# Long convolution over 256 positions: second half kept reversed, no mirror product, inverse products of 128 columns, even and odd parts combined on VectorE

## Chip, cores and metric

One core of one Trainium2 chip runs the whole program. The metric is the device time of one execution in microseconds (us). The kernel before took 1390.03 us (median of three executions, 1386.08 to 1390.8).

## The reference, cut to what matters

The program computes two trunk layers on 128 prompt tokens and 256 sample tokens. Layer 0 mixes the tokens by a state-space scan and, beside it, by an order-2 "Hyena": a short convolution gives three parts of 1024 channels each, and two long convolutions over the whole sequence are gated by parts 1 and 2:

```python
def long_conv(u, h, bias):
    L = u.shape[1]
    U = jnp.fft.rfft(uf, n=2 * L, axis=1)
    Hf = jnp.fft.rfft(h.astype(jnp.float32), axis=0)
    y = jnp.fft.irfft(U * Hf[None], n=2 * L, axis=1)[:, :L]
    return (y + uf * bias.astype(jnp.float32)).astype(u.dtype)
...
    parts = jnp.split(dwconv_centred(hy, hy_conv_w, hy_conv_b), 1 + HY_ORDER, axis=-1)
    filters = hyena_filters(L, hy_w1, hy_b1, hy_w2, hy_b2, hy_w3, hy_freq)
    u = parts[0]
    for o in range(HY_ORDER):
        u = parts[o + 1] * long_conv(u, filters[:, o], hy_bias[o])
    return jnp.concatenate([y, u], axis=-1) @ w_out, final
```

After it come the output projection, a mixture of experts (router, gather, 16 pairs of experts), a second layer of attention, and a second mixture of experts.

## The kernel before

Data are held with channels on partitions: `u0T`, `p1T` and `hyT` are the three Hyena parts, eight chunks of 128 channels by 384 positions (prompt 0 to 127, sample 128 to 383). The program is written out per engine; semaphores are counted. `bank_plan` (L115) lists in TensorE's order every result that goes through one of the 8 PSUM banks, with the engine that takes it out; `open_bank` (L841) makes TensorE wait until the bank's former content is taken, `full` and `took` (L632, L636) are the waits for "TensorE has finished this job" and "its taker has read it". All matmuls are issued by `mm` (L851) and all transposes by `tr` (L855), so the profile shows them under these two lines. A float32 `mm` is two recorded MATMULs, a `tr` is one. `link` issues an instruction on VectorE and waits for its end before the next; a plain instruction is not waited for.

The long convolution is done by products with constant cosine matrices, in four turns, one for each (half of the channels b, order o) in `HYO`: (0,0), (1,0), (0,1), (1,1). Per turn TensorE does this (L1125 to L1187, loop L1227):

- `spectrum`: 6 products of 512 columns from the token-major inputs `ut` (2 for the prompt, 4 for the sample);
- for the next turn `tokens` (12 transposes into banks 6, 7 and again 6, which ScalarE copies to `ut`) and `filters` (6 products, copied out by ScalarE and then multiplied by a decay on GpSimd, L2636), and among the filters `mirror`: one product of 512 columns with a flipped identity, that reverses the second sample half;
- `prompt_back`: 8 products of 128 columns, once VectorE has the prompt's spectrum (`spec`);
- for the next turn `prompt_response`: 2 products of 512 columns;
- `sample_back`: 16 products of 256 columns into banks 2 and 3, once VectorE has all three spectra;
- for the next turn `sample_response`: 4 products of 512 columns.

VectorE per turn (L2325): `spectrum` three times (6 instructions on 128x512, L2307 to L2313), `mirror` (L2275, L2276: second half plus and minus the first), `gate` on the prompt (L2320), `prompt_response` (L2281), `gate` twice on the sample, one for each bank, and `sample_response` (5 instructions, L2285 to L2295). In the last turn TensorE has no next turn to prepare and does `first_states`, 16 products of the output projection, in that place.

Ahead of the turns, 24 chunks of the Hyena projection are convolved with three taps on VectorE (L2248 to L2251; the third tap is one instruction per segment). SyncE's queue starts the first expert weights when jobs of the last turn are done (`LAST_UTK` L742, `LAST_SPEC_S`, `LAST_INV` L758), the rest as experts are used (L770); GpSimd's queue waits for `LAST_INV` at L2639.

Of the kernel before, what the change touches and what calls it, by code (L numbers as in the profile page):

```python
# [114 lines left out]
def bank_plan():  # L115
# [81 lines left out]
    def tokens(b, o):  # L197
        for t, bank in ((0, 6), (2, 7), (1, 6)):
            job(("utk", b, o, t), "act", None, bank)

    def filters(b, o):
        for i, (s, x, t) in enumerate(HY_FILTERS):
            job(("PQ", b, o, s, x, t), "act", None, (7, 6, 1)[i % 3])
            if i == 0 and (b, o) != HYO[0]:
                job(("rev", b, o), "dve", None, 0)

    for turn in range(-1, len(HYO)):
        if turn >= 0:
            b, o = HYO[turn]
            for s in range(2):  # L210
                for k in range(s + 1):
                    job(("U", b, o, s, k, 0), "none", None, 2 * (s + k))
                    job(("U", b, o, s, k, 1), "dve", None, 2 * (s + k) + 1)
            if turn + 1 < len(HYO):
                tokens(*HYO[turn + 1])
                filters(*HYO[turn + 1])
            job(("inv", b, o, 0, 0), "dve", None, 7)
        else:
            tokens(*HYO[0])
        if turn + 1 < len(HYO):  # L220
            job(("H", *HYO[turn + 1], 0), "dve", None, 6)
            job(("H", *HYO[turn + 1], 1), "act", None, 1)
            if turn < 0:
                job(("rev", *HYO[0]), "dve", None, 0)
# [129 lines left out]
def host_constants():  # L354
# [15 lines left out]
    def halves(n):  # L370
# [9 lines left out]
        back = [w.T / (2 * n) for pair in both for w in pair]  # L380
# [8 lines left out]
    def feat(n):  # L389
# [29 lines left out]
            "k_slots": slots, "k_small": small, "k_rev": rev, "k_flip": rev / 8, "k_pick": pick}  # L419
# [5 lines left out]
def build_kernel(nc, A, K, outs):  # L425

    with ExitStack() as ctx:
# [103 lines left out]
        dft = area(16384, 2560)  # L531
        dft0 = dft[:, 0:512].rearrange("p (x n) -> p x n", x=4)
        dft1 = dft[:, 512:1536].rearrange("p (x n) -> p x n", x=8)
        dft1_back = dft[:, 1536:2560].rearrange("p (x n) -> p x n", x=4)
# [6 lines left out]
        flip = hyl[0][:, 3584:3584 + P]  # L541
# [85 lines left out]
        def wide(h):  # L627
            return slice(h * 512, (h + 1) * 512)
        done = S("pe_done")
# [208 lines left out]
        def _(pe):  # L838
# [286 lines left out]
            def tokens(b, o):  # L1125
# [3 lines left out]
                for t in (0, 2, 1):  # L1129
# [5 lines left out]
            def mirror(b, o):  # L1135
                ps = open_bank("rev", b, o)
                took(pe, "utk", b, o, 2)
                mm(ps[:, :], flip, ut[:, 2, :], True, True).then_inc(done, 1)

            def filters(turn, b, o):  # L1140
                for i, (s, x, t) in enumerate(HY_FILTERS):
                    ps = open_bank("PQ", b, o, s, x, t)
                    mm(ps[:, :], (hsP, hsQ)[x][:, cols(s + t)], w3s[:, b, o, :], True, True).then_inc(done, 1)
                    if i == 0 and turn:
                        mirror(b, o)
# [13 lines left out]
            def spectrum(b, o):  # L1159
# [4 lines left out]
                took(pe, "rev", b, o)  # L1164
# [13 lines left out]
            def sample_back(turn, b, o):  # L1178
                pe.wait_ge(S("spec"), 3 * turn + 3)
                for i in range(2):  # L1180
                    ps = open_bank("inv", b, o, 1, i)
                    for c in range(2):
                        for k in range(2):
                            for x in range(2):
                                last = mm(ps[:, c * LS:(c + 1) * LS], yspec[1 + k][:, x, cols(2 * i + c)], dft1_back[:, 2 * k + x, :],
                                          k == x == 0, k == x == 1)
                    last.then_inc(done, 1)  # L1187

            for q in range(3):
                for c in range(KD):  # L1190
# [19 lines left out]
                    if ("hy", q, c) == FILTERS_AFTER:  # L1210
                        pe.wait_ge(S("hs"), 1)
                        pe.wait_ge(S("hypar0_in"), 16 * 6)
# [12 lines left out]
            mirror(*HYO[0])  # L1225
# [345 lines left out]
        def _(act):  # L1571
# [197 lines left out]
            for c in range(3 * KD):  # L1769
# [13 lines left out]
                if (c // KD, c % KD) == GATES_AFTER:  # L1783
# [4 lines left out]
                    for l in range(2):  # L1788
                        act.dma_start(gates_d[l].rearrange("g v (c p) -> c (g v) p", p=P),
                                      gstage[0:KD, l, :].rearrange("c (i p) -> c i p", p=P)).then_inc(S("gates_out"), 16)  # L1790
            act.wait_ge(S("gates_out"), 16 * 2)
            for turn, (b, o) in enumerate(HYO):
                for t in (0, 2, 1):
# [11 lines left out]
                A_(gsin, bank("G", b, o, 2)[:, :], ACT.Copy).then_inc(taken["act"], 1)  # L1805

# [190 lines left out]
        def _(dve):  # L1997
# [245 lines left out]
            for c in range(3 * KD):  # L2243
# [72 lines left out]
            def gate(b, o, s, i):  # L2316
                full(dve, "inv", b, o, s, i)
                c, n = (b * 4, 4) if s == 0 else (b * 4 + 2 * i, 2)
                dst = (p1T if o == 0 else hyT)[:, c:c + n, SEGS[s][0]:SEGS[s][1]]
                take(TT(dst, dst, bank("inv", b, o, s, i)[:, :].rearrange("p (c n) -> p c n", c=n), mult))  # L2320
# [4 lines left out]
            for turn, (b, o) in enumerate(HYO):  # L2325
# [6 lines left out]
                gate(b, o, 0, 0)  # L2332
# [242 lines left out]
        def _(pool):  # L2575
# [53 lines left out]
            pool.wait_ge(S("hypar0_in"), 16 * 6)  # L2629
# [159 lines left out]
```

## Time and profile before

| | |
|---|---|
| median of three executions | 1390.03 us |
| lowest, highest | 1386.08, 1390.8 us |
| span of the profiled execution, first to last instruction | 1382.9 us |
| device time of the profiled execution itself | not given beside its span |
| TensorE busy over the span | 88% |
| VectorE, ScalarE, GpSimd busy | 33%, 24%, 14% |

The span leaves out what lies around the first and the last instruction: the median is 7.1 us above it, the lowest time 3.2 us. A row of a timeline gives start, duration, engine, line, operation, "output<-inputs" by buffer name, and count; a bracket gives the idle time before it and what ended that. Merged rows (x12) are of equal instructions in a row. `arena`, `ring`, `hT`, `scr`, `rstd` are regions of SBUF, `bank` is PSUM.

### The profile page before, as it was taken

The numbers are of one execution on the slowest core, as the hardware profiler recorded it, in microseconds if no ns is written. First come the engines' busy times: TensorE is split into PE (matmuls) and PEld (weight loads), VectorE is DVE, ScalarE is ACT, GpSimd is POOL, SyncE is SP. The second block draws the span as 40 slices with busy tenths as digits, with TensorE's granted clock in tenths as the row PEclk, the third lists the DMA queues.
The fourth block names the chain that finished last, engine by engine and source line by source line (L and its number), as shares of the span: only waits on it lengthen the run. The fifth ranks groups of instructions, "written<-read, shape, count | busy, mean of one in ns | idle before, by whom it ended". The sixth has DMA issues, their size and how long they took to land.

```text
span 1382.9 us, 16600 instructions
## 1 busy us (share of the span) xinstructions
PE 1221.0 (88%) x6381; PEld 689.0 (50%) x6381; DVE 457.1 (33%) x958; ACT 329.9 (24%) x843; POOL 191.6 (14%) x253
## 2 busy tenths in 40 slices
PE   3999998999989999959999875999888969989773
PEld 2456654454545664446555441853455446545431
DVE  1452078542338850241111114212363331111105
ACT  4112364210122200231111113313353221111103
POOL 1000022200123401011221200152001011212100
PEclk9999999999999999979999997999999979999996
DMA  9995510666910118259999995950314469999983
GB/s 332 323 387 209 182 31 1 225 242 248 349 60 1 61 51 332 83 180 391 418 418 417 420 411 222 354 56 7 137 62 124 182 229 416 419 419 419 419 369 146
DMA packets 94417, 337.23 MB, mean 244 GB/s; under 512 B 12784, under 2 KB 16598, under 8 KB 69649
## 3 DMA queue, kind: packets, MB, share of 16 engines
q1 hardware_dynamic: 73472, 303.18, 56.2%
q0 software_dynamic: 13984, 26.19, 6.8%
q10 hardware_dynamic: 6897, 6.97, 1.5%
q8 instruction: 45, 0.74, 0.2%
q14 instruction: 19, 0.16, 0.0%
HBM read 334.08 MB, written 23.18 MB: 258 GB/s over the span
## 4 chain that ended last, share of the span: by engine, by line
PE 71%; DMA 17%; DVE 6%; ACT 3%; issue 2%; POOL 1%; SPq 0%; ACTq 0%; DVEq 0%; POOLq 0%
PE bank L851 63%; DMA ring<-in_moe_w_down_dram 10%; PE bank L855 5%; DMA ring<-in_moe_w_up_dram 3%; PE bank L882 3%; DMA arena<-expert_rows 1%; DMA xR<-in_x_sample_dram 1%; DVE arena L2477 1%; PE bank L948 1%; ACT ring L1963 1%; DVE arena L2480 1%; DMA hT<-rows,scr 0%; DMA arena<-in_hy_freq_dram 0%; ACT rstd L1598 0%; DMA expert_rows<-arena,scr 0%
## 5 line engine op out<-in xcount | busy, mean ns | idle before, releaser
L851 PE MATMUL bank<-ring,arena 128*64 128x256 f32 (+3 forms) x2624 | 438.5, 439 | 43.9 <-DMA ring<-in_moe_w_up_dram 17.4
L851 PEld LDWEIGHTS bank<-ring,arena 128*64 128x64 f32 (+1 forms) x2624 | 218.2, 146 | 229.8 <-issue 120.2
L851 PE MATMUL bank<-hT,ring 128*128 128x384 f32 (+5 forms) x968 | 306.1, 474 | 4.3 <-ACT hT L1670 3.6
L851 PEld LDWEIGHTS bank<-hT,ring 128*128 128x128 f32 (+1 forms) x968 | 180.1, 193 | 125.7 <-issue 19.1
L851 PE MATMUL bank<-arena 128*64 128x256 f32 (+7 forms) x800 | 117.2, 383 | 11.2 <-DVE arena L2425 4.5
L2452 DVE TENSOR_TENSOR hT<-hT,bank 128x256 f32<-128x256 f32 x32 | 13.5, 421 | 266.8 <-ACT hT L1850 266.8
L851 PEld LDWEIGHTS bank<-arena 128*64 128x64 f32 (+4 forms) x800 | 60.2, 150 | 53.4 <-issue 29.6
L1850 ACT ACTIVATE hT<-bank 128x256 f32<-128x256 f32 x32 | 12.3, 384 | 248.4 <-PE bank L851 248.4
L855 PEld LDWEIGHTS bank<-cst,hT 128*128 128x128 f32 x368 | 47.4, 190 | 48.0 <-issue 35.9
L855 PE MATMUL bank<-cst,hT 128*128 128x128 f32 x368 | 61.1, 301 | 11.3 <-DMA hT<-rows,scr 11.3
L855 PE MATMUL bank<-cst,arena 128*128 128x128 f32 (+3 forms) x207 | 31.9, 302 | 37.7 <-ACT arena L1611 19.3
L851 PE MATMUL bank<-ring,hT 128*128 128x512 f32 x144 | 62.7, 594 | 0.4 <-ACT hT L1977 0.4
L851 PE MATMUL bank<-arena,ring 128*128 128x256 f32 (+3 forms) x272 | 60.0, 373 | 3.2 <-ACT arena L1926 1.8
L2457 DVE COPY arena<-bank 128x512 f32<-128x512 f32 x32 | 22.1, 691 | 111.6 <-PE bank L851 111.6
L851 PEld LDWEIGHTS bank<-arena,ring 128*128 128x128 f32 (+2 forms) x272 | 41.5, 184 | 23.9 <-issue 9.2
L855 PEld LDWEIGHTS bank<-cst,arena 128*128 128x128 f32 (+3 forms) x207 | 26.5, 157 | 48.5 <-issue 39.9
L851 PE MATMUL bank<-arena,cst 128*128 128x512 f32 (+5 forms) x76 | 37.2, 645 | 12.4 <-DVE arena L2398 9.4
L1861 ACT ACTIVATE arena<-bank 128x512 f32<-128x512 f32 x32 | 19.1, 597 | 114.6 <-PE bank L851 114.6
L851 PEld LDWEIGHTS bank<-ring,hT 128*128 128x128 f32 x144 | 27.1, 190 | 33.8 <-issue 33.2
L2675 POOL DMA_INDIRECT hT<-rows,scr x32 | 33.0, 1030 | 71.8 <-PE bank L855 27.9
L2691 POOL COPY scr<-arena 128x1 int32 x28 | 5.1, 183 | 271.1 <-ACT arena L1861 164.5
L2681 POOL DMA_INDIRECT expert_rows<-arena,scr x32 | 32.7, 1020 | 59.8 <-POOL scr L2691 23.5
(305 smaller groups left out, 1120.2 us busy)
## 6 DMA issues: line engine op xcount, KB each, us to landing
ring<-in_moe_w_up_dram SPq DMA_DIRECT2D x28, 2048.0 KB, 21.0
ring<-in_moe_w_down_dram SPq DMA_DIRECT2D x28, 2048.0 KB, 20.1
ring<-in_w_ada_dram SPq DMA_DIRECT2D x24, 2048.0 KB, 15.2
ring<-in_moe_w_gate_dram SPq DMA_DIRECT2D x24, 2048.0 KB, 21.0
ring<-in_ev_w_in_dram SPq DMA_DIRECT2D x11, 2048.0 KB, 11.7
arena<-in_moe_w_gate_dram SPq DMA_DIRECT2D x8, 2048.0 KB, 14.4
ring<-in_ev_w_out_dram SPq DMA_DIRECT2D x4, 2048.0 KB, 15.8
arena<-in_moe_w_up_dram SPq DMA_DIRECT2D x4, 2048.0 KB, 19.0
```

Of the source, the lines that this page charges most:

```text
L851: return nc.tensor.matmul(out, lhsT, rhs, start=start, stop=stop_, skip_group_check=True)
L855: return nc.tensor.transpose(out, in_, ident[0:n, 0:n])
L882: last = nc.tensor.matmul(ps[32 * g:32 * g + 32, :], conds[l][:, k, at:at + 32], w[:, k, :], start=b == first and k < 4, stop=(l, b) in AD ...
L948: last = nc.tensor.matmul(ps[32 * q:32 * q + 32, :], conds[0][:, k, 22 - 2 * j:54 - 2 * j], w[:, k, :], start=j == 0 and k < 4, stop=j == ...
L1861: A_(ob[:, 0:512], banks[5][:, :], ACT.Copy).then_inc(s["d_act"], 1)
L1963: A_(prob[b][:, a, 0:w], bank("score", n, a)[:, 0:w], ACT.Exp, bias=nrows[:, b, 1, a:a + 1], scale=scale, accum_out=nrows[:, b, 2, a:a + 1 ...
L2452: TT(hid[:, b, :], sg[:, b, :], banks[2 + b][:, HID:2 * HID], mult).then_inc(s["hid"], 1)
L2457: COPY(ob[:, 512:1024], banks[6][:, :]).then_inc(s["d_dve"], 1)
L2477: link(STT(out=y0, in0=y1, scalar=ysw[:, NT + t:NT + t + 1], in1=y0, op0=mult, op1=add))
L2480: weighed = TT(y0, y0, bank("gff", l, v, h), mult)
L2675: nc.gpsimd.indirect_dma_start(xs[:, b, :], None, rows_d[l], bass.IndirectOffsetOnAxis(ap=at, axis=0), bounds_check=T - 1, oob_is_err=False)\
L2681: nc.gpsimd.indirect_dma_start(outs_d[l], bass.IndirectOffsetOnAxis(ap=idxc[:, 2 + b:3 + b], axis=0), ob, None, bounds_check=2 * T - 1, oo ...
```

## The change

The sample's second half of parts 0 and 1 is written backwards by the third tap of the short convolution, which becomes three instructions. So no mirror product is needed: the middle block of tokens is transposed in the place where `mirror` stood, into bank 0, and VectorE adds and subtracts straight from it. The even and the odd frequencies' inverse products are kept apart (8 products of 128 columns each): ScalarE copies the odd part to the new region `mirrored`, and VectorE forms even+odd (first half) and even-odd (second half, reversed) and multiplies each with the gate, for o = 1 through an access pattern that walks backwards. The constant `k_flip` and its DMA go, and half of the inverse matrices.

```diff
     def tokens(b, o):
-        for t, bank in ((0, 6), (2, 7), (1, 6)):
+        for t, bank in ((0, 6), (2, 7)):
...
             if i == 0 and (b, o) != HYO[0]:
-                job(("rev", b, o), "dve", None, 0)
+                job(("utk", b, o, 1), "dve", None, 0)
...
-                job(("inv", b, o, 1, i), "dve", None, 2 + i)
+                job(("inv", b, o, 1, i), ("act", "dve")[i], None, 2 + i)
...
-        back = [w.T / (2 * n) for pair in both for w in pair]
+        back = [w[:h].T / (2 * n) for pair in both for w in pair]
...
+        def backwards(ap):
+            step, n = ap.ap[-1]
+            return bass.AP(ap.tensor, ap.offset + step * (n - 1), [*ap.ap[:-1], [-step, n]])
...
-            def mirror(b, o):
-                ps = open_bank("rev", b, o)
-                took(pe, "utk", b, o, 2)
-                mm(ps[:, :], flip, ut[:, 2, :], True, True).then_inc(done, 1)
+            def middle_tokens(b, o):
+                src = u0T if o == 0 else p1T
+                ps = open_bank("utk", b, o, 1)
+                for c in range(4):
+                    last = tr(ps[:, cols(c)], src[:, b * 4 + c, cols(1)])
+                last.then_inc(done, 1)
...
-                    for c in range(2):
+                    for c in range(4):
                         for k in range(2):
-                            for x in range(2):
-                                last = mm(ps[:, c * LS:(c + 1) * LS], yspec[1 + k][:, x, cols(2 * i + c)], dft1_back[:, 2 * k + x, :],
-                                          k == x == 0, k == x == 1)
+                            x = (k + 1 - i) % 2
+                            last = mm(ps[:, cols(c)], yspec[1 + k][:, x, cols(c)], dft1_back[:, 2 * k + x, :], k == 0, k == 1)
...
+            def take_odd(b, o):
+                full(act, "inv", b, o, 1, 0)
+                A_(mirrored, bank("inv", b, o, 1, 0)[:, :], ACT.Copy).then_inc(taken["act"], 1)
...
                 A_(him[0], bank("H", b, o, 1)[:, :], ACT.Copy).then_inc(taken["act"], 1)
+                if turn:
+                    take_odd(*HYO[turn - 1])
                 full(act, "G", b, o, 2)
...
-                for v, (a, b) in enumerate(SEGS):
-                    last = STT(out=dst[:, a:b], in0=src[:, 2 + a + v:2 + b + v], scalar=col("hy_conv_w", 6 * KD + c),
-                               in1=acc[:, a + v:b + v], op0=mult, op1=add)
+                for v, (a, b) in enumerate(SEGS if q == 2 else (SEGS[0], (LP, 2 * P), (2 * P, T))):
+                    to, v = dst[:, a:b], min(v, 1)
+                    last = STT(out=backwards(to) if q < 2 and a == 2 * P else to, in0=src[:, 2 + a + v:2 + b + v],
+                               scalar=col("hy_conv_w", 6 * KD + c), in1=acc[:, a + v:b + v], op0=mult, op1=add)
...
             def mirror(b, o):
-                full(dve, "rev", b, o)
-                took(dve, "utk", b, o, 1)
-                ps = bank("rev", b, o)[:, :]
-                link(TT(ut[:, 2, :], ut[:, 1, :], ps, sub))
-                take(TT(ut[:, 1, :], ut[:, 1, :], ps, add))
+                full(dve, "utk", b, o, 1)
+                took(dve, "utk", b, o, 2)
+                ps = bank("utk", b, o, 1)[:, :]
+                link(TT(ut[:, 1, :], ps, ut[:, 2, :], add))
+                take(TT(ut[:, 2, :], ps, ut[:, 2, :], sub))
...
+            def sample_gate(b, o):
+                full(dve, "inv", b, o, 1, 1)
+                took(dve, "inv", b, o, 1, 0)
+                even = bank("inv", b, o, 1, 1)[:, :]
+                dst = (p1T if o == 0 else hyT)[:, 4 * b:4 * b + 4, :]
+                near, far = dst[:, :, cols(1)], dst[:, :, cols(2)]
+                if o == 1:
+                    far = backwards(far)
+                link(TT(ytmp[:, :], even, mirrored, add))
+                link(TT(mirrored, even, mirrored, sub))
+                TT(near, near, by_chunk(ytmp[:, :]), mult)
+                take(TT(far, far, by_chunk(mirrored), mult))
...
-                for i in range(2):
-                    gate(b, o, 1, i)
+                sample_gate(b, o)
...
-                    dma(flip, K["k_flip"]).then_inc(S("hypar0_in"), 16)
```

## Rows read from the trace of the kernel before

**Rows 1.** The page: span, and busy time of each engine.

```profile
span 1382.9 us, 16600 instructions
...
PE 1221.0 (88%) x6381; PEld 689.0 (50%) x6381; DVE 457.1 (33%) x958; ACT 329.9 (24%) x843; POOL 191.6 (14%) x253
```

**Rows 2.** Window, one turn: length, busy of each engine, PEclk, DMA, GB/s.

```profile
415.97:442.94 26.97, 26.72 (x100) 16.27 (x98) 21.48 (x30) 6.46 (x11) 8.39 (x6) 1.00 0.00 1
```

**Rows 3.** Timeline, TensorE and ScalarE, first turn.

```profile
415.97 1.04 PE L855 MATMUL bank<-cst,arena 128*128 128x128 f32 x8
...
416.61 1.09 ACT L1795 ACTIVATE hT<-bank 128x512 f32<-128x512 f32 x2 [5.85 <-PE bank L855]
...
417.75 1.12 PE L851 MATMUL bank<-ring,arena 128*128 128x512 f32 x2
...
418.71 1.02 PE L851 MATMUL bank<-hT,ring 128*128 128x512 f32 x2
...
419.57 4.45 PE L851 MATMUL bank<-ring,arena 128*128 128x512 f32 x10
...
423.86 1.95 PE L851 MATMUL bank<-arena,ring 128*128 128x128 f32 x16
...
425.64 1.88 PE L851 MATMUL bank<-hT,arena 128*128 128x512 f32 x4
...
427.36 7.16 PE L851 MATMUL bank<-arena,ring 128*128 128x256 f32 x32
...
434.36 3.60 PE L851 MATMUL bank<-arena 128*128 128x512 f32 x8
...
437.79 5.31 PE L851 MATMUL bank<-hT,arena 128*128 128x512 f32 x12
```

**Rows 4.** Timeline, VectorE, first turn.

```profile
412.84 0.69 DVE L2307 TENSOR_TENSOR ring<-bank,hT 128x512 f32<-128x512 f32 x1 [0.33 <-PE bank L851]
...
416.93 0.69 DVE L2307 TENSOR_TENSOR ring<-bank,arena 128x512 f32<-128x512 f32 x1
...
425.74 1.55 DVE L2313 TENSOR_TENSOR ring<-ring,rstd 128x512 f32<-128x512 f32 x1
427.32 0.69 DVE L2275 TENSOR_TENSOR hT<-hT,bank 128x512 f32<-128x512 f32 x1
428.05 0.69 DVE L2276 TENSOR_TENSOR hT<-hT,bank 128x512 f32<-128x512 f32 x1
428.65 0.68 DVE L2320 TENSOR_TENSOR arena<-arena,bank 128x512 f32<-128x512 f32 x1
...
434.56 0.69 DVE L2320 TENSOR_TENSOR arena<-arena,bank 128x512 f32<-128x512 f32 x1 [2.77 <-PE bank L851]
```

**Rows 5.** Timeline, the entry into the first turn.

```profile
403.30 0.65 PE L855 MATMUL bank<-cst,arena 128*128 128x128 f32 x4 [0.31 <-ACT hT L1795]
...
404.74 1.10 PE L851 MATMUL bank<-scr,arena 128*128 128x512 f32 x2 [0.78 <-ACT hT L1795]
```

**Rows 6.** One line's instructions: L2309 on VectorE; GpSimd's timeline in the first turn.

```profile
L2309 DVE TENSOR_TENSOR ring<-ring,rstd x12: 691/692/1602, 414.2 to 503.2; 128x512 f32<-128x512 f32 x12
...
422.55 5.87 POOL L2636 TENSOR_TENSOR arena<-arena,ring 128x512 f32<-128x512 f32 x4
```

**Rows 7.** Timeline, last turn; a chunk of the short convolution.

```profile
496.83 13.90 PE L851 MATMUL bank<-ring,arena 128*128 128x512 f32 x32
...
309.30 0.48 DVE L2248 TENSOR_SCALAR arena<-arena,par 128x385 f32<-128x385 f32 x1 [3.24 <-ACT arena L1755]
```

**Rows 8.** SyncE's queue; windows behind the turns (columns as in rows 2).

```profile
621.62 0.37 SPq L765 DMA_DIRECT2D arena<-in_moe_w_gate_dram  x1
...
760.00:822.00 62.00, 49.55 (x360) 26.73 (x356) 6.73 (x13) 6.93 (x16) 9.16 (x15) 1.00 1.01 418
610.00:620.00 10.00, 2.17 (x73) 2.04 (x72) 4.71 (x19) 0.00 (x0) 2.12 (x2) 0.50 0.12 34
990.00:1000.00 10.00, 8.61 (x70) 5.67 (x68) 6.82 (x21) 5.36 (x20) 0.00 (x0) 1.00 0.33 96
```

More of the change, by code:

```diff
@@ L530, in build_kernel @@
         hacc = area(13072, 2, PADDED - 2)
-        dft = area(16384, 2560)
+        dft = area(16384, 2048)
         dft0 = dft[:, 0:512].rearrange("p (x n) -> p x n", x=4)
         dft1 = dft[:, 512:1536].rearrange("p (x n) -> p x n", x=8)
-        dft1_back = dft[:, 1536:2560].rearrange("p (x n) -> p x n", x=4)
+        dft1_back = dft[:, 1536:2048].rearrange("p (x n) -> p x n", x=4)
+        mirrored = area(18432, 512)
         hsP, hsQ = area(18944, T), area(19328, T)
@@ L540, in build_kernel @@
         hyb = hyl[1][:, 0:2048].rearrange("p (b o n) -> p b o n", b=2, o=2)
-        flip = hyl[0][:, 3584:3584 + P]
         hy_lent = ring[:, HY_LENT * SLOT:(HY_LENT + 1) * SLOT]
@@ L1128, in tokens @@
                     took(pe, "inv", b, 0, 1, 1)
-                for t in (0, 2, 1):
+                for t in (0, 2):
                     ps = open_bank("utk", b, o, t)
@@ L1144, in filters @@
                     if i == 0 and turn:
-                        mirror(b, o)
+                        middle_tokens(b, o)
             def prompt_response(turn, b, o):
@@ L1163, in spectrum @@
                     mm(ps[:, :], dft0[:, x, :], ut[:, 0, :], True, True).then_inc(done, 1)
-                took(pe, "rev", b, o)
+                took(pe, "utk", b, o, 1)
                 for k in range(2):
@@ L1211, in _ @@
                         pe.wait_ge(S("hs"), 1)
-                        pe.wait_ge(S("hypar0_in"), 16 * 6)
+                        pe.wait_ge(S("hypar0_in"), 16 * 5)
                         filters(0, *HYO[0])
@@ L1224, in _ @@
             prompt_response(0, *HYO[0])
-            mirror(*HYO[0])
+            middle_tokens(*HYO[0])
             sample_response(0, *HYO[0])
@@ L1790, in _ @@
                                       gstage[0:KD, l, :].rearrange("c (i p) -> c i p", p=P)).then_inc(S("gates_out"), 16)
+            def take_odd(b, o):
+                full(act, "inv", b, o, 1, 0)
+                A_(mirrored, bank("inv", b, o, 1, 0)[:, :], ACT.Copy).then_inc(taken["act"], 1)
             act.wait_ge(S("gates_out"), 16 * 2)
             for turn, (b, o) in enumerate(HYO):
-                for t in (0, 2, 1):
+                for t in (0, 2):
                     full(act, "utk", b, o, t)
@@ L1805, in _ @@
                 A_(gsin, bank("G", b, o, 2)[:, :], ACT.Copy).then_inc(taken["act"], 1)
+            take_odd(*HYO[-1])
             def moe(l):
@@ L2314, in spectrum, with by_chunk, prompt_gate @@
                 dve.wait_ge(S("spec"), 3 * turn + i + 1)
[L2316 to L2320, printed above, removed]
+            def by_chunk(ap):
+                return ap.rearrange("p (c n) -> p c n", c=4)
+            def prompt_gate(b, o):
+                full(dve, "inv", b, o, 0, 0)
+                dst = (p1T if o == 0 else hyT)[:, 4 * b:4 * b + 4, cols(0)]
+                take(TT(dst, dst, by_chunk(bank("inv", b, o, 0, 0)[:, :]), mult))
+            def sample_gate(b, o):
[10 more added lines that the diff above has]
+                take(TT(far, far, by_chunk(mirrored), mult))
             prompt_response(*HYO[0])
@@ L2331, in _ @@
                     mirror(*HYO[turn + 1])
-                gate(b, o, 0, 0)
+                prompt_gate(b, o)
                 if more:
                     prompt_response(*HYO[turn + 1])
-                for i in range(2):
-                    gate(b, o, 1, i)
+                sample_gate(b, o)
                 if more:
@@ L2627, in _ @@
                 dma(decay[b], K["k_decay"][:, :, b * 512:(b + 1) * 512].rearrange("t p n -> p t n")).then_inc(S("hypar%d_in" % which), 16)
-            pool.wait_ge(S("hypar0_in"), 16 * 6)
+            pool.wait_ge(S("hypar0_in"), 16 * 5)
             for turn, (b, o) in enumerate(HYO):
```

4 lines of the change are left out of this document (2 added, 2 removed).

## The prediction

> **What bounds the kernel now.** I read the page's engine line first: TensorE is busy 88% of the span, VectorE 33% [rows 1]. So a product taken away on TensorE is worth its time, unless something else is late in that place. The place is the four turns of the long convolution, and the windows by turn come next: a turn is 26.97 us long and TensorE is busy 26.7 of it, while VectorE is busy 21.5 [rows 2]. The reader is to see that VectorE has only 5.5 us of room in a turn, and that the change gives work to it. The timelines of one turn then show who waits for whom: in the first turn VectorE finishes its last spectrum at 425.74+1.55 = 427.29 [rows 4] and TensorE starts the sample's inverse products at 427.36 [rows 3], which is also where its own preceding products end (425.64 + 4 x 0.43). The two engines arrive together. After that VectorE waits for TensorE, 2.77 us in one piece before the second sample gate [rows 4].
>
> **The change on TensorE.** A stage ends where the next row starts, since the ends of matmuls are modelled.
>
> Inverse products: 32 passes of 256 columns from 427.36 to 434.36, 7.00 us, 0.219 each [rows 3]. After: 16 products are again 32 passes, but of 128 columns. The trace has this very form, with the same operands' regions, in the prompt's inverse: 16 passes from 423.86 to 425.64, 1.78 us, 0.111 each [rows 3]. So 3.56 us, 3.44 less in each of four turns, 13.76 in all. The Trainium skill (TensorE: Matmul & The Clock Gate, Back-to-back issue gap) gives about 81 ns for one of a stream of 128-column matmuls; the row has 111 ns for a float32 pass. By the page these 32 passes would take 2.6 us and a turn would save 0.96 more where TensorE binds. I go by the row.
>
> Mirror: it occupies 418.71 to 419.57, 0.86 us [rows 3]. In its place come 4 transposes; eight take 1.04 us and four 0.65, both with the same tail [rows 3, 5], so four are about 0.41. That is 0.45 less. The place they leave among the tokens gives nothing: the first filter product goes into bank 7 and needs ScalarE's second copy, which ends at 416.61+1.09 = 417.70, and it starts at 417.75 [rows 3]. It will start then with or without the middle transposes.
>
> Entry to the first turn: the middle transposes start at 403.30, after a wait for ScalarE's copy, and the first response product at 404.74, again after a wait for a copy [rows 5]. Without them the response product can start at 403.30: 1.44 less, and 0.45 for the mirror, 1.89.
>
> If all that counted, the sum would be 13.76 + 3 x 0.45 + 1.89 = 17.0 us.
>
> **The change on VectorE.** Call T the start of the sample's inverse products. Before, VectorE gates the first bank while the second is computed. After, the gate needs both parts, so it waits for the last product; behind it stand, in order, the next turn's sample response and its three spectra, and for the last spectrum waits TensorE's next T. That is a loop through both engines:
> - product seen at T + 3.56 + 0.20 (before: 434.36 to 434.56 [rows 3, 4]);
> - four instructions in place of two: an instruction that is waited for takes 0.72 to the next start, one that is not 0.60 (427.32, 428.05, 428.65 [rows 4]): 2 x 0.72 + 2 x 0.60 = 2.64. The last two multiply SBUF by SBUF, which no gate did before; nearest rows 0.69 us alone and 1.60 beside GpSimd [rows 6]. GpSimd ends its six products about 1 us after T (422.55+5.87 = 428.42 against 427.36 [rows 3, 6]), before they start. I take 0.60;
> - sample response: five instructions by the same step of 0.72, 3.60, if TensorE doesn't hold it up; it does so before, not after, as its four products start at T + 3.56 already;
> - three spectra. One alone takes 412.84 to 416.93, 4.09, three 12.3; the trace has 14.45 (412.84 to 427.29) [rows 4], since L2309 and L2313 read two SBUF operands and take up to 1.55 to 1.60 instead of 0.69 while GpSimd works [rows 4, 6]. The Trainium skill (SBUF — State Buffer, Who interferes with whom) has the rule: a VectorE instruction with two SBUF inputs and a GpSimd instruction that reads SBUF exclude each other, and the later waits for the whole of the other; these rows agree with it. The cost now is three hits, 2.15 us. After, the spectra of turns 1 and 2 start later against TensorE's filters, so GpSimd starts about 5.8 us after them and not 6.8. Six GpSimd products of 1.25 let one VectorE instruction in after every two, so again three hits, but each with nearly a full wait of 0.95: 15.1 us. Bounds: no hit 12.3, all six instructions hit 18.0;
> - 0.07 until TensorE starts.
>
> Sum 3.76 + 2.64 + 3.60 + 15.1 + 0.07 = 25.2 us, against 26.97 before: 1.78 less per turn. TensorE itself would be ready at T + 3.56 (inverse) + 3.43 (response) + 5.15 (434.36 and 437.79 to 442.94 [rows 2, 3]) + 1.78 (tokens until the first filter) + 0.86 + 0.41 + 4.29 + 1.78 + 1.72 = 23.0. So TensorE, gapless before, will wait about 2.2 us before the inverse products of turns 1 and 2.
>
> By turns, from the first T to the end:
> - turn 0: its spectra start when TensorE's first product pair is done, 1.89 earlier (VectorE is ready 0.2 before). With GpSimd's second product 0.45 earlier they take some 0.35 longer, 14.8: T comes 1.5 earlier;
> - turns 1 and 2: 2 x 1.78 = 3.56;
> - from turn 2's T to the end of turn 3: two inverse stages shorter, 6.88. Here `first_states`, 32 passes from 496.83 to 510.56 [rows 7], covers VectorE, whose spectra without GpSimd end at about T + 22.3, before TensorE asks at T + 26.
>
> Sum 1.5 + 3.56 + 6.88 = 11.9, taken as **12 us**.
>
> **Edits at nothing.** ScalarE's copy of the odd part (0.60) starts at T + 2.0 and is over at T + 2.6, while the gate waits until T + 3.76 for the even part; behind it on ScalarE stands only the sine copy, whose product is done at T + 6.1. If the copy were late the gate would wait for it one for one. The third tap in three pieces adds one VectorE instruction, 0.35 to 0.5 us, to 16 chunks, where VectorE is idle 3.24 us in a chunk [rows 7]; a write that walks backwards is in no row, its bounds being the 0.35 of a forward one and the longest row, 1.60, both under the idle time. The backward gates of o = 1 (turns 2 and 3) stand ahead of work that `first_states` or the output projection covers. The Trainium skill (DVE: opcode table, Instruction layouts) allows negative steps and gives no price. The flip DMA and the smaller matrix shorten a queue nobody waits for. `LAST_UTK` moves behind one filter product, 0.9 us later for a load into an empty queue.
>
> **What comes behind.** SyncE issues the next loads when jobs of the last turn are done, and the load at 621.62 after the gather; both follow TensorE and move with it [rows 8]. From there the DMA queues are full, share 1.01 at 418 GB/s while TensorE has gaps [rows 8]. Such a stretch has a fixed length but starts when it is triggered, so I count the 12 us in full behind it.
>
> On the profiled execution's span of 1382.9 this is 1370.9; the median stands 7.1 above the span: 1390.0 - 12.0 = **1378.0 us**.
>
> **Rivals.**
> 1. TensorE stays the bound: if contention with GpSimd vanishes (spectra 12.3, loop 22.4 under TensorE's 23.0), all 17.0 count: 1373.0. For it: VectorE is idle 5.5 us per turn. Against: that idle time lies behind TensorE's long inverse, which goes. Chance 0.14.
> 2. Given back later: the expert weights set the end of the mixture, and if their transfers can't start earlier a large part of the 12 goes. For it: share 1.01. Against: every trigger moves. With two thirds lost, 1386. Chance 0.12.
> 3. Contention at its worst, all six hits: loop 28.1, 1.1 more per turn, turn 0 1.7 more, and 6.88 saved: 3.0 less, 1387. It needs GpSimd busy in the whole of the spectra; its six products fill half. Chance 0.05.
> 4. Slower: the clock. TensorE's new waits of about 2 us could drop its granted clock to 1.2 GHz, as in the window 610 to 620, where it was busy 2.17 of 10 us and was granted 0.50 [rows 8]. If the 7.0 us of inverse and response behind each of three waits ran at half speed they would cost 21 in all: 1399. It decides from 4 us per turn on. Against: between 990 and 1000, with 1.4 us of waits in it (busy 8.61 of 10), the granted clock is 1.00 [rows 8]. The Trainium skill (TensorE: Matmul & The Clock Gate, Part 1) says that the clock follows how busy TensorE has been, so this is the rule that speaks against the change. Chance 0.05.
>
> **Numbers.** The forecast has 0.64, with 1375.5 to 1381 as its own range. The range 1373 to 1384 takes in rival 1, most of the bounds of the contention, and part of rival 2. Within 0.3% (4.2 us) a change can't be told from none. Faster: the forecast, rival 1 and about half of rival 2, 0.85; same: the rest of 2 and rival 3, 0.10; slower 0.05.
>
> **What would show it.** Right: sample inverse products 32 passes in 3.6 us; TensorE waiting for L2313's successor about 2 us in turns 1 and 2, about 1 in turn 0 and none in turn 3; turns of about 25 us; VectorE with hardly any idle time but the wait for the even part. Wrong: passes at 0.219, turns of 23 us or of over 26, a granted clock below 1.00 between 400 and 510, or a wait for weights behind 700 that has grown by as much as was saved.

## Result and the profile after

| | before | after |
|---|---|---|
| median | 1389.4 us (4 runs, 1386.08 to 1390.8) | 1375.79 us (4 runs, 1373.8 to 1378.57) |
| ratio | | 0.99, 95% interval 0.9873 to 0.9926 |
| profiled execution: device time / span | not given / 1382.9 | 1374.37 / 1372.4 us |
| TensorE, VectorE busy over the span | 88%, 33% | 88%, 34% |

The change is faster by 13.6 us of medians, 1.0%, and the interval of the ratio leaves out 1; a second set of runs, below, gave 0.9904 (0.9887 to 0.992). The forecast was 1378.0. The two profiled spans lie only 10.5 us apart. The median of before stands 6.5 above its span, while a single execution's time lies about 2 us above its own span (1374.37 over 1372.4; 1.6 to 3.1 in all executions that have both). So some 4.5 us between span and median of before was spread between executions: its profile comes from one of the shorter ones.

To see where the time comes from, the stage of the four turns is measured by the starts of TensorE's rows, which the spread of the rest of the program does not touch. As in the prediction, T is the start of a turn's sample inverse products, and the entry is the way from the first token transposes to the first turn's spectrum. The columns: whole stage, from its first token transposes to the end of its last inverse product; T0, from the same start to the first T; the next two turns, T to T; the rest; and the lowest granted clock in windows of 2 us over the entry.

| kernel | stage | T0 | turns | rest | clock |
|---|---|---|---|---|---|
| before | 117.36 | 25.46 | 26.97, 26.95 | 37.98 | 1.00 |
| after | 106.43 | 25.36 | 24.87, 24.85 | 31.35 | 0.50 |

The first view is the timeline of after, TensorE, from the entry to the second turn. `mm` is now L855 and `tr` L859.

```profile
401.29 1.09 PE L859 MATMUL bank<-cst,arena 128*128 128x128 f32 x8 [2.66 <-DVE arena L2264]
402.78 1.52 PE L855 MATMUL bank<-scr,arena 128*128 128x512 f32 x2 [0.40 <-ACT hT L1804]
404.10 1.91 PE L855 MATMUL bank<-rstd,arena 128*128 128x512 f32 x2
405.80 1.06 PE L859 MATMUL bank<-cst,arena 128*128 128x128 f32 x4
...
426.65 3.84 PE L855 MATMUL bank<-arena,ring 128*128 128x128 f32 x32 [0.24 <-DVE ring L2326]
430.33 3.60 PE L855 MATMUL bank<-arena 128*128 128x512 f32 x8
433.76 5.31 PE L855 MATMUL bank<-hT,arena 128*128 128x512 f32 x12
438.92 1.04 PE L859 MATMUL bank<-cst,arena 128*128 128x128 f32 x8
440.69 1.12 PE L855 MATMUL bank<-ring,arena 128*128 128x512 f32 x2 [0.74 <-ACT hT L1804]
...
451.52 2.72 PE L855 MATMUL bank<-arena,ring 128*128 128x128 f32 x22 [1.47 <-DVE ring L2326]
```

The reader is to see three things. The 32 inverse passes of 128 columns take 430.33 - 426.65 = 3.68 us where [rows 3] had 7.00. A wait for VectorE stands before them, 1.47 us in turn 1 (0.24 in turn 0), where before the two engines arrived together. And at the entry the products run at half speed: the second response product's two passes of 512 columns take 405.80 - 404.10 = 1.70 us from start to start, and in the kernel before 0.86:

```profile
405.67 1.02 PE L851 MATMUL bank<-rstd,arena 128*128 128x512 f32 x2
406.53 1.02 PE L851 MATMUL bank<-hT,ring 128*128 128x512 f32 x2
```

VectorE in after, from the gate of turn 0 to the last spectrum of turn 1:

```profile
430.53 0.69 DVE L2345 TENSOR_TENSOR rstd<-bank,arena 128x512 f32<-128x512 f32 x1 [1.28 <-PE bank L855]
...
432.59 0.68 DVE L2348 TENSOR_TENSOR arena<-arena 128x512 f32<-128x512 f32 x1
433.19 0.68 DVE L2298 TENSOR_TENSOR ring<-bank,ring 128x512 f32<-128x512 f32 x1
...
436.56 0.68 DVE L2320 TENSOR_TENSOR ring<-bank,hT 128x512 f32<-128x512 f32 x1
...
444.02 1.62 DVE L2326 TENSOR_TENSOR ring<-ring,rstd 128x512 f32<-128x512 f32 x1
...
447.00 1.55 DVE L2322 TENSOR_TENSOR ring<-ring,rstd 128x512 f32<-128x512 f32 x1
...
449.92 1.55 DVE L2326 TENSOR_TENSOR ring<-ring,rstd 128x512 f32<-128x512 f32 x1
451.50 0.69 DVE L2288 TENSOR_TENSOR hT<-bank,hT 128x512 f32<-128x512 f32 x1
```

From 430.53 to 451.50 VectorE never stops, and three instructions that read two SBUF operands take 1.55 to 1.62 us in place of 0.69. Such a long one is called a hit below. The windows of the same kernel, turns 1 and 2 and the rest (length, busy of TensorE, weight load, VectorE, ScalarE, GpSimd, granted clock, DMA):

```profile
426.65:451.52 24.87, 22.66 (x97) 13.37 (x97) 22.97 (x32) 6.87 (x12) 9.45 (x7) 1.00 0.00 1
451.52:476.37 24.85, 22.65 (x96) 13.36 (x97) 22.95 (x32) 6.47 (x11) 8.35 (x6) 1.00 0.23 85
476.37:507.72 31.35, 31.35 (x132) 18.91 (x133) 20.98 (x32) 2.76 (x4) 0.00 (x0) 1.00 0.07 21
```

Against [rows 2] TensorE is no longer busy all the time (22.66 of 24.87; the 2.21 us are 1.47 of waiting for VectorE and 0.74 for ScalarE's copy of the tokens), with the granted clock at 1.00 all the same. The last window is gapless.

### The profile page after: what moved, and what is told of

It is laid out like the page before. It is cut to its first block, busy times and chain, and to the rows that moved or that the text cites. A ratio compares the mean times of both kernels' runs of the same rounds, so it can differ in the third digit from the quotient of the medians.

```text
span 1372.4 us, 16607 instructions
## 1 busy us (share of the span) xinstructions
PE 1206.8 (88%) x6373; PEld 677.9 (49%) x6373; DVE 464.7 (34%) x982; ACT 329.9 (24%) x843; POOL 191.3 (14%) x252
## 4 chain that ended last, share of the span: by engine, by line
PE 68%; DMA 17%; DVE 9%; ACT 3%; issue 2%; POOL 1%; SPq 0%; ACTq 0%; DVEq 0%; POOLq 0%
PE bank L855 60%; DMA ring<-in_moe_w_down_dram 10%; PE bank L859 5%; DMA ring<-in_moe_w_up_dram 4%; PE bank L886 3%; DMA arena<-expert_rows 1%; DVE ring L2326 1%; DVE ring L2322 1%; DMA xR<-in_x_sample_dram 1%; PE bank L952 1%; ACT ring L1975 1%; DMA hT<-rows,scr 0%; ACT rstd L1603 0%; DVE rstd L2324 0%; DVE ring L2320 0%
## 5 line engine op out<-in xcount | busy, mean ns | idle before, releaser
L855 PE MATMUL bank<-ring,arena 128*64 128x256 f32 (+3 forms) x2624 | 438.1, 438 | 46.4 <-DMA ring<-in_moe_w_up_dram 17.8
L855 PEld LDWEIGHTS bank<-ring,arena 128*64 128x64 f32 (+1 forms) x2624 | 217.7, 146 | 230.8 <-issue 117.9
L855 PE MATMUL bank<-hT,ring 128*128 128x384 f32 (+4 forms) x960 | 302.9, 474 | 4.3 <-ACT hT L1675 3.6
L855 PEld LDWEIGHTS bank<-hT,ring 128*128 128x128 f32 (+1 forms) x960 | 178.6, 193 | 123.9 <-issue 17.2
L855 PE MATMUL bank<-arena 128*64 128x256 f32 (+7 forms) x800 | 117.3, 383 | 10.6 <-DVE arena L2452 4.5
L855 PEld LDWEIGHTS bank<-arena 128*64 128x64 f32 (+4 forms) x800 | 60.0, 151 | 52.1 <-issue 29.1
L859 PEld LDWEIGHTS bank<-cst,hT 128*128 128x128 f32 x368 | 47.4, 190 | 48.1 <-issue 35.9
L859 PE MATMUL bank<-cst,hT 128*128 128x128 f32 x368 | 61.1, 301 | 11.4 <-DMA hT<-rows,scr 11.4
L859 PE MATMUL bank<-cst,arena 128*128 128x128 f32 (+3 forms) x207 | 32.7, 308 | 37.0 <-ACT arena L1616 19.8
L855 PE MATMUL bank<-ring,hT 128*128 128x512 f32 x144 | 63.2, 597 | 0.4 <-ACT hT L1989 0.4
L855 PE MATMUL bank<-arena,ring 128*128 128x128 f32 (+2 forms) x272 | 46.8, 324 | 6.4 <-DVE ring L2326 3.2
L859 PEld LDWEIGHTS bank<-cst,arena 128*128 128x128 f32 (+3 forms) x207 | 27.6, 160 | 49.5 <-issue 42.8
L855 PE MATMUL bank<-arena,cst 128*128 128x512 f32 (+5 forms) x76 | 36.4, 632 | 12.4 <-DVE arena L2425 9.4
L855 PEld LDWEIGHTS bank<-ring,hT 128*128 128x128 f32 x144 | 27.3, 192 | 34.3 <-issue 33.5
L855 PEld LDWEIGHTS bank<-arena,ring 128*128 128x128 f32 (+2 forms) x272 | 32.1, 185 | 24.6 <-issue 9.2
## 6 DMA issues: line engine op xcount, KB each, us to landing
ring<-in_w_ada_dram SPq DMA_DIRECT2D x24, 2048.0 KB, 15.1
```

Of the source, the lines that this page charges most:

```text
L855: return nc.tensor.matmul(out, lhsT, rhs, start=start, stop=stop_, skip_group_check=True)
L859: return nc.tensor.transpose(out, in_, ident[0:n, 0:n])
```

## The experiments

Eleven runs, all with a profile. The totals of single executions scatter by some 5 us (the four spans of after ran from 1371.9 to 1376.6) and do not follow the stage from run to run, so the stage is what the experiments are read by; a second run of after gave the stage as 106.44 and its turns as 24.85 and 24.87. The last column is the total; it is a median of 5 executions for "all" and of 6 for "after again", and a single execution elsewhere.

| kernel | stage | T0 | turns | rest | clock at the entry | total |
|---|---|---|---|---|---|---|
| inverse only | 104.67 | 25.46 | 23.92, 23.94 | 31.35 | kept | 1375.0 |
| reversed only | 118.10 | 26.27 | 26.90, 26.91 | 38.02 | fell | 1388.89 |
| small decay | 100.79 | 23.29 | 23.13, 23.13 | 31.24 | kept | 1375.16 |
| filled entry | 104.77 | 23.68 | 24.87, 24.87 | 31.35 | kept | 1376.33 |
| spectrum in PSUM | 102.48 | 24.97 | 23.13, 23.13 | 31.25 | fell | 1371.11 |
| dummy in mirror's place | 104.08 | 24.87 | 23.92, 23.94 | 31.35 | fell | 1379.44 |
| all | 98.26 | 22.44 | 22.29, 22.28 | 31.25 | kept | 1368.32 |
| after again | 106.44 | 25.37 | 24.85, 24.87 | 31.35 | fell | 1375.12 |
| PSUM and filler | 100.79 | 23.28 | 23.13, 23.13 | 31.25 | kept | 1374.49 |
| mirror kept, PSUM | 104.73 | 26.39 | 23.55, 23.55 | 31.24 | fell | 1372.67 |
| before again | 118.24 | 26.38 | 26.95, 26.94 | 37.97 | fell | 1387.49 |

### Half of the change each: inverse only, reversed only

The first keeps the natural order and the mirror product, and takes only the split inverse with its gate; the second stores the half reversed and keeps the old inverse of 256 columns. Both cuts are against the kernel after.

```diff
# inverse only
...
-                if o == 1:
-                    far = backwards(far)
+                far = backwards(far)
...
# reversed only
...
-                    for c in range(4):
+                    for c in range(2):
                         for k in range(2):
-                            x = (k + 1 - i) % 2
-                            last = mm(ps[:, cols(c)], yspec[1 + k][:, x, cols(c)], dft1_back[:, 2 * k + x, :], k == 0, k == 1)
+                            for x in range(2):
+                                last = mm(ps[:, c * LS:(c + 1) * LS], yspec[1 + k][:, x, cols(2 * i + c)], dft1_back[:, 2 * k + x, :],
+                                          k == x == 0, k == x == 1)
...
```

> The inverse products of 128 columns, ScalarE's copy and the four-instruction gate alone; storage and mirror product as before. Measure: the stage from the first token transpose to the end of the last inverse product, 117.36 us before and 106.43 after the whole change. Theory A (turns 1 and 2 are bound by the loop through VectorE, TensorE's time is free there; the mirror's place is worth nothing): turns of 24.9 us, first inverse stage at 25.5 as before, the rest 31.35, sum about 106.6, so the whole change again. Rival B (TensorE's time counts one for one): 117.36 - 13.76 = 103.6, and the mirror's removal would be worth more beside it.

> The reversed storage alone: no mirror product, middle tokens in its place; inverse products of 256 columns and gates by bank as before (for o = 1 a gate is two instructions, one of them backwards). Theory A: VectorE's last spectrum comes no earlier in a turn, so turns stay at 26.9 to 27.0 us with TensorE waiting about 0.5; only the entry can gain, 0.1 to 1.9 by whether its clock falls: stage 115.4 to 117.2. Rival B (one for one): another 1.35, stage 114.1 to 115.9, turns of 26.5.

Inverse only measured 104.67 us for the stage: the whole change's gain and 1.8 us more. Reversed only measured 118.10, turns of 26.90 against 26.97: nothing from the reversal alone. TensorE's saved 0.43 us turns into waiting, as VectorE's last spectrum comes no earlier (the row before the inverse products shows 0.18 us of it). The turns are as expected; the stage is not (115.4 to 117.2): the clock fell at its entry, and earlier than in after, so that the first eight transposes take 1.97 us and not 1.09, and T0 is 0.81 above that of before. For inverse only the theory had put the stage at 106.6 and its rival at 103.6; 104.67 is neither. A VectorE that works as in after would have made turns of 24.87, and they are 23.92. VectorE in its turn 1:

```profile
444.90 0.69 DVE L2324 TENSOR_TENSOR ring<-ring,rstd 128x512 f32<-128x512 f32 x1
...
446.95 1.55 DVE L2320 TENSOR_TENSOR ring<-ring,rstd 128x512 f32<-128x512 f32 x1
...
449.87 1.54 DVE L2324 TENSOR_TENSOR ring<-ring,rstd 128x512 f32<-128x512 f32 x1
```

Two hits, not three, and the turn is 24.87 - 23.92 = 0.95 us shorter, which is about what one hit adds (1.62 - 0.69 = 0.93). GpSimd tells why. First inverse only, then after:

```profile
443.40 1.27 POOL L2660 TENSOR_TENSOR hT<-hT,ring 128x512 f32<-128x512 f32 x1 [14.79 <-ACT hT L1769]
445.12 1.60 POOL L2660 TENSOR_TENSOR hT<-hT,ring 128x512 f32<-128x512 f32 x1 [0.45 <-ACT hT L1769]
```

```profile
442.53 2.57 POOL L2662 TENSOR_TENSOR hT<-hT,ring 128x512 f32<-128x512 f32 x2 [14.79 <-ACT hT L1770]
445.05 5.86 POOL L2662 TENSOR_TENSOR arena<-arena,ring 128x512 f32<-128x512 f32 x4
```

With the mirror product between the first two filter products the second filter comes late enough for GpSimd to pause 0.45 us. VectorE's instruction at 444.90 starts in the pause and runs in 0.69, and GpSimd's product is the one held (1.60, not 1.27). Without the mirror product GpSimd's first two products join, and VectorE's instruction at 444.02 waits. The dummy, below, tests this.

### Is it GpSimd: small decay, and the spectrum through PSUM

Small decay runs GpSimd's decay on 8 of the 512 columns in turns 1 to 3 (the rest of the decay is left out). Spectrum in PSUM keeps all of GpSimd's work, but two products of the spectrum are written back into their PSUM bank, so that no addition reads two SBUF operands (two waits of TensorE that go with it are not shown). It also has one wait of VectorE less per spectrum.

```diff
-                    nc.gpsimd.tensor_tensor(at, at, decay[b][:, s + t, :], ALU.mult)
+                    w = slice(0, 8) if turn else slice(0, 512)
+                    nc.gpsimd.tensor_tensor(at[:, w], at[:, w], decay[b][:, s + t, w], ALU.mult)
# spectrum in PSUM, all six instructions
+                TT(y0, u0, hre[i], mult)
+                TT(y1, u1, hre[i], mult)
+                TT(u0, u0, him[i], mult)
+                link(TT(u1, u1, him[i], mult))
+                TT(y1, y1, u0, add).then_inc(S("spec"), 1)
+                take(TT(y0, y0, u1, sub))
...
```

> After, with GpSimd's decay product of turns 1 to 3 done on 8 of 512 columns only (the decay is left out on the others). Theory A with contention: VectorE's two-SBUF-operand instructions all take 0.69, three spectra 12.3 us, the loop falls under TensorE's 23.0: turns of 23.0 us, stage about 102.5. Rival C (the loop is long for another reason than GpSimd): the slow instructions stay at 1.55 or the turns at 24.9, stage 106.4.

> After, with the six instructions of a spectrum rewritten: two of the four products go back in place into PSUM, so that the sum and the difference read one SBUF and one PSUM operand, with one wait less. The same work on GpSimd as in after. Theory A' (the loop through VectorE binds turns 1 and 2, and what stretches it is two-SBUF-operand instructions beside GpSimd): every instruction at 0.7 us although GpSimd works as long as before, a spectrum 3.7 us, turns of 23.1 us as with the small decay product, stage 100.8 us at full clock (102.5 if the clock falls at the entry). Rival (GpSimd slows VectorE whatever the operands): instructions of 1.5 us stay, turns of 24 to 25, stage 104 to 106.

Both give turns of 23.13 us and no hit on VectorE; small decay does so with the six instructions of after, so the wait saved is not the cause. Two rows of spectrum in PSUM, then GpSimd at full work beside them:

```profile
444.40 0.69 DVE L2324 TENSOR_TENSOR bank<-bank,arena 128x512 f32<-128x512 f32 x1
...
445.73 0.69 DVE L2326 TENSOR_TENSOR ring<-ring,bank 128x512 f32<-128x512 f32 x1
```

```profile
444.01 4.99 POOL L2663 TENSOR_TENSOR arena<-arena,ring 128x512 f32<-128x512 f32 x4
```

GpSimd gains too: its last four products take 4.99 us, not the 5.86 of after. 23.13 is TensorE's own time (in both runs its waits in the turns are for ScalarE's copies alone, 0.74 per turn), so contention decides in after: the three held instructions add 0.93 + 0.86 + 0.86 = 2.65 us to VectorE's loop, which without them (22.2) would be done before TensorE asks, and push it 1.74 past TensorE's time. The Trainium skill (SBUF — State Buffer, Who interferes with whom) says that a VectorE instruction with at most one SBUF input, outside the 2-port modes, doesn't contend with GpSimd, and that issue order decides which of two blocks the other; both are seen in these rows, the first here, the second in the 1.60 of inverse only.

### A dummy product in the mirror's place

After, with one useless product of 256 columns (0.43 us) ahead of the middle transposes.

```diff
                 ps = open_bank("utk", b, o, 1)
+                if (b, o) != HYO[0]:
+                    mm(ps[:, 0:256], ident, dft[:, 0:256], True, True)
```

> After, with a product of 256 columns (0.43 us, result overwritten) ahead of the middle transposes of turns 1 to 3, so that they take 0.86 us together, as the mirror product did. Theory F (without the mirror product GpSimd's second product follows the first without a gap, and a third VectorE instruction is caught behind it; the inverse products alone had two caught and turns of 23.9): added work on TensorE makes the turns shorter, 23.9 to 24.0 instead of 24.9, stage 1.9 us shorter, 104.5 (102.9 at full clock). Rival (turns differ for another reason): turns stay at 24.9.

The turns fall to 23.92 and 23.94, by 0.95 and 0.91, exactly as in inverse only, and VectorE has two hits: TensorE does more and the turn is shorter. GpSimd pauses again:

```profile
441.73 1.27 POOL L2664 TENSOR_TENSOR hT<-hT,ring 128x512 f32<-128x512 f32 x1 [14.79 <-ACT hT L1772]
443.46 1.61 POOL L2664 TENSOR_TENSOR hT<-hT,ring 128x512 f32<-128x512 f32 x1 [0.46 <-ACT hT L1772]
```

### The entry: filler, and the kernel before once more

Filled entry gives TensorE three useless products of 512 columns (2.7 us) in the 2.66 us in which it waits for the short convolution, ahead of the first tokens.

```diff
...
+            for _ in range(3):
+                mm(banks[BANK[JOB[("utk", *HYO[0], 1)]]], ident, dft[:, 0:512], True, True)
             pe.wait_ge(S("hconv"), 3 * KD)
             tokens(*HYO[0])
```

> After, with three products of 512 columns into a free bank while TensorE waits for the last chunk of the short convolution (2.6 us of work in an idle time of 2.66, result not used). Theory D (the entry gained 0.1 us where 1.5 was forecast because the granted clock fell to half from 403 to 407, behind the idle time): clock 1.00 throughout, response products 0.43 a pass instead of 0.85, first inverse stage 1.6 us earlier, stage 104.8. Rival E (the fall has nothing to do with the idle time, or the entry is bound by VectorE): stage stays at 106.4.

> The kernel before once more, for the clock at the entry: 1.00 from 398 to 412 and a stage of 117.4 us if the old order of the entry keeps the clock up; 0.88 or lower and a stage above 118 if the fall comes by chance in every kernel without filler.

T0 falls from 25.36 to 23.68, 1.68 us, and the turns stay. The windows over the entry, first after, then filled entry:

```profile
402.00:404.00 2.00, 1.60 (x6) 0.73 (x5) 0.00 (x0) 1.09 (x2) 0.00 (x0) 0.83 0.00 0
404.00:406.00 2.00, 2.00 (x4) 0.76 (x3) 0.69 (x1) 0.00 (x0) 0.00 (x0) 0.50 0.00 0
406.00:408.00 2.00, 2.00 (x9) 1.28 (x8) 1.06 (x2) 0.60 (x1) 0.00 (x0) 0.81 0.00 0
```

```profile
402.00:404.00 2.00, 1.78 (x10) 0.86 (x8) 0.72 (x2) 0.47 (x1) 0.00 (x0) 1.00 0.00 0
404.00:406.00 2.00, 1.73 (x4) 0.82 (x5) 0.50 (x1) 0.61 (x2) 0.00 (x0) 1.00 0.00 0
406.00:408.00 2.00, 2.00 (x9) 1.20 (x8) 1.46 (x3) 0.60 (x1) 0.00 (x0) 1.00 0.00 0
```

In after the granted clock falls to the lower level, 1.2 GHz (0.50), behind TensorE's 2.66 us of idleness. That the filler works through the clock alone is seen in small decay, which has none and kept 1.00: from the first transposes to the first spectrum product it takes 408.45 - 401.28 = 7.17 us, filled entry 409.93 - 402.77 = 7.16, after 410.13 - 401.29 = 8.84. Is it the change that makes the clock fall? The kernel before, run again, says no: the same idle time and the same fall.

```profile
402.90 2.98 PE L855 MATMUL bank<-cst,arena 128*128 128x128 f32 x12 [2.66 <-DVE arena L2251]
```

```profile
402.00:404.00 2.00, 1.10 (x5) 1.10 (x6) 0.81 (x3) 0.00 (x0) 0.00 (x0) 0.61 0.00 0
404.00:406.00 2.00, 1.88 (x9) 1.18 (x7) 0.00 (x0) 1.28 (x3) 0.00 (x0) 0.54 0.00 0
```

Its twelve transposes take 2.98 us there and T0 is 26.38, not 25.46: the fall costs it 0.9 us, and costs after 1.7. Counting every profile, the clock fell in 7 of 10 without filler (after twice, before once of two, reversed only, both with a PSUM spectrum alone, the dummy) and kept in 3 (before, inverse only, small decay); with filler it kept in 3 of 3. That the filler holds the clock up is likely on these numbers, not shown; what decides without it stays open.

### Together, and the price of the mirror once TensorE binds

```diff
# all: PSUM spectrum and filler as above, and in bank_plan
...
+                    if s and k and turn + 1 < len(HYO):
+                        job(("utk", *HYO[turn + 1], 0), "act", None, 6)
...
-            job(("PQ", b, o, s, x, t), "act", None, (7, 6, 1)[i % 3])
+            job(("PQ", b, o, s, x, t), "act", None, (6, 7, 1)[i % 3])
...
```

> Spectrum in PSUM and the three filler products at the entry, nothing else. Theory D (the idle time ahead of the entry lets the clock fall): clock 1.00 from 398 to 412, stage 100.8 us (102.5 without the filler). Rival E (the fall comes by chance, filler or not): in some of such runs the clock is 0.88 in this window, stage 102.5. The step from here to the version with all edits is then the copies no longer waited for, 100.8 to 98.3.

> Natural storage with the mirror product, inverse products of 128 columns, and the spectrum in PSUM. It asks what the mirror product costs once VectorE no longer binds. Theory A': TensorE binds, and the mirror costs its 0.43 us a turn more than the transposes: turns of 23.56 instead of 23.13. Rival (its place is free in any case, as it was beside a binding VectorE): turns of 23.13. The entry is that of the kernel before, clock 1.00 if the old order is what keeps it up: stage about 103.3.

> After, with the spectrum in PSUM, the three filler products at the entry, the first filter product in bank 6 and the first token block transposed ahead of the last two spectrum products, so that no copy is waited for. By theory A' TensorE binds all turns: 22.1 us each, first inverse stage at 22.4 us, stage about 97.8 us, 6 to 7 us below after at full clock, total some 20 us (1.4%) below before. If VectorE still bound turns 1 and 2: turns of 23 and more, stage 100 or more.

> The changed kernel again, unchanged, beside the others on one chip: 0.99 of before (0.987 to 0.993). Turns 24.9 us in every execution; at the entry the granted clock either falls (stage 106.4) or not (104.8).

PSUM and filler add up: 100.79, with T0 23.28 and turns of 23.13. Mirror kept (inverse only with the PSUM spectrum) has turns of 23.55, 0.42 above 23.13: as soon as VectorE doesn't bind, the mirror costs its price on TensorE in full (0.45 predicted), and no more. "All" also transposes the first token block earlier, between the spectrum's products, which takes away the 0.74 us of waiting for ScalarE's copy:

```profile
435.69 0.60 PE L861 MATMUL bank<-cst,arena 128*128 128x128 f32 x4
436.13 1.88 PE L857 MATMUL bank<-hT,arena 128*128 128x512 f32 x4
437.85 0.60 PE L861 MATMUL bank<-cst,arena 128*128 128x128 f32 x4
438.28 1.02 PE L857 MATMUL bank<-ring,arena 128*128 128x512 f32 x2
```

Its window over 30 us of the turns:

```profile
442.00:472.00 30.00, 30.00 (x141) 18.68 (x140) 26.82 (x43) 9.25 (x17) 13.00 (x11) 1.00 0.19 70
```

TensorE is busy 30.00 of 30.00, turns are 22.29 and the stage 98.26. Its median is 1368.32 us (5 runs, 1365.63 to 1370.18), a ratio of 0.9853 (0.9834 to 0.9871) to before; after, beside it, 1375.12 (6 runs) and 0.9904 (0.9887 to 0.992). The intervals don't meet: this version beats both. Of the 8.2 us of the stage 6.8 show in the medians.

## Why the prediction was right, and where by luck

Right in time and mostly by its own steps. With the entry's clock alike in both, the stage is 117.36 - 104.77 (filled entry) = 12.6 us shorter at full clock, and 118.24 - 106.44 = 11.8 where it fell; the sum had said 11.9. Between the first two profiles, where the clock fell in after alone, it is 10.9. That the errors of the sum partly cancel is luck: the two turns gave 4.20 us where 3.56 was forecast, and the fall of the clock, which the sum did not have, took most of the entry's gain. Step by step:

- **Inverse passes.** 3.44 less per turn predicted. Measured 3.68 us (3.57 where no wait stands before them, in spectrum in PSUM) for 7.00. The two last ones: 37.98 - 31.35 = 6.63, predicted 6.88.
- **The loop through VectorE**, 25.2 predicted, 24.87 measured, by its terms, with the forecast in brackets: product seen 3.88 (3.76), gate 2.66 (2.64), sample response 3.37 (3.60), spectra 14.91 (15.1), start 0.05 (0.07). TensorE ready at T + 23.4 (23.0). The wait of 1.47 was predicted as 2.2. Three hits, of 0.93, 0.86 and 0.86 (three of 0.95), and no rise to six: rival 3 is out, and rival 1 (TensorE the bound) too; small decay shows what a turn would have been under it, 23.13.
- **Mirror.** Here the working, though not the sum, had a hole. Removing the mirror product was counted as 0.45 per turn for TensorE and so, inside a loop in which VectorE binds, as nothing in turns 1 and 2. That it also shifts GpSimd's second product was seen for turn 0 alone (0.35 us there). The three hits per turn were foreseen, as a matter of when the spectra start, and measured; but in turns 1 and 2 the third of them comes from the mirror's removal, since inverse only and the dummy have two. The removal therefore cost 0.95 in each of these turns, which eats the 1.78 gained at the entry: the stage of inverse only (104.67) equals that of the whole change at full clock (104.77). The expectation for inverse only, turns of 24.9, missed for the same reason. The forecast was spared because it counted three hits for the whole change and never split it.
- **Entry.** 1.5 us predicted; 25.46 - 25.36 = 0.1 measured between the first two profiles. In filled entry, at full clock, it is 25.46 - 23.68 = 1.78, and TensorE waits 0.24 us for VectorE before the first T, where about 1 was predicted. The term was right in the main; what came in between was the clock's fall, which strikes before as well. A granted clock below 1.00 between 400 and 510 had been named as a sign of being wrong, and it appeared (0.50 in 404 to 406). Rival 4 spoke of the clock and placed the fall behind the new waits, where it stayed at 1.00; at the entry, with its 2.66 us of idleness, I had not looked for one.
- **Edits at nothing.** No cost of them is seen. ScalarE's copy of the odd part runs from T + 2.1 to T + 2.7 (428.74 to 429.34), before the gate at T + 3.9. VectorE is still idle 3.24 us before the last chunk of the short convolution. A gate that writes backwards takes what a forward one takes (L2348, turn 2, against 0.68 at 432.59):

```profile
482.31 0.69 DVE L2348 TENSOR_TENSOR arena<-arena 128x512 f32<-128x512 f32 x1
```

- **Behind the stage.** The full shift was predicted. The load after the gather is issued 621.62 - 609.98 = 11.64 us earlier for a stage that ends 11.54 earlier, and the span ends 10.5 earlier:

```profile
609.98 0.37 SPq L769 DMA_DIRECT2D arena<-in_moe_w_gate_dram  x1
```

So the mixture, full of transfers as it is [rows 8], took back little: inside it equal loads are issued 10.8 to 11.4 us earlier, and at 968 us 10.97. Rival 2 is out. Behind it the lead shrinks to 9.5 at 1122 and is 10.5 at the end; what takes that in the attention stage was not tried, and with one profile each it can be scatter.
- **The total.** 12 was predicted and the stage gives 11.8 to 12.6; the medians give 13.6, with an interval of 10.3 to 17.6 (0.0074 and 0.0127 of 1389.4), which holds both. The 2.7 us by which the medians moved more than the profiled stage (10.9) lie inside the scatter of the rest of the program; no run says more. The forecast came out 2.2 us high, 0.6 of it because the median of before is now 1389.4. Of the 7.1 us that were said to lie around the span only about 2 do, and the rest is spread between executions; as they were added on both sides, the sum did not suffer.

## What to carry to other kernels

When a product is taken off the engine that binds, write down the loop through the next engine first, term by term: here the loop through VectorE left 2.1 us per turn (26.97 to 24.87) of the 3.84 that TensorE alone would have given (to 23.13). Before counting a removed instruction as harmless, ask which third engine's start it was holding apart. And if VectorE and GpSimd work side by side, look for VectorE instructions with two SBUF operands (0.69 alone, up to 1.62 beside GpSimd) and route one operand through PSUM, which here cost no instruction.

## What the hardware showed that was not expected

- Adding 0.43 us of useless work to TensorE shortened a turn by 0.95 us, through a pause of 0.46 us that it opened on GpSimd.
- A VectorE product written in place into the PSUM bank that it read took 0.69 us, as one into SBUF, and GpSimd's four products got 0.87 us shorter for it.
- The same kernel, with the same 2.66 us of idleness, was granted 1.00 in one profile and 0.50 in another: 25.46 against 26.38 us to the first inverse.
